# Second pass of a hybrid decoder step: stages that end without GpSimd's drain, the samples' selection in pieces, two expert steps inside the gating's norm

## The reference

```python
proj = x @ w_in                                  # z, xbc, dt, uv, gates
y_a = ssd_branch(z, xbc, dt, ...)                # causal conv, chunked state-space scan, gated RMS norm
u, v = split(gelu(uv)); v = layer_norm(v)        # the gating branch
y_b = u * (tril(w_s) @ v + b_s)                  # spatial gating in chunks of 128 tokens
g_a, g_b = split(sigmoid(gates))
mix = (g_a * (y_a @ w_a) + g_b * (y_b @ w_b)) @ w_out
h = layer_norm(ALPHA * x + mix)
# PEER: 8 heads, product keys: top 16 of 128 on either side, top 16 of their 256 sums
expert, gate = ...                               # 8 * 16 = 128 experts per token, softmax weights
act = gelu(einsum('td,thkd->thk', h, peer_u[expert]))
x = layer_norm(ALPHA * h + einsum('thk,thkd->td', gate * act, peer_v[expert]))
```

## Time and profile before

| | |
|---|---|
| median of 3 runs | 5216.41 us (5214.78 to 5218.38) |
| the profiled execution: first to last instruction (span) | 5205.6 us |
| busy share of the span: PE, PEld, DVE, ACT, POOL | 87, 65, 54, 16, 43% |
| moved by DMA | 1674.51 MB, 322 GB/s over the span |

### The profile page before, as it was taken

One profiled execution on the slowest core, in us unless ns is written; L12 is line 12 of the kernel. 1 busy time (PEld: TensorE's weight loads), 2 busy tenths in 40 slices (PEclk: granted clock), 3 DMA queues, 4 the chain that ended last, 5 costly groups with the idle time before them and its releaser, 6 DMA issues. The chain is left out here.

```text
span 5205.6 us, 48526 instructions
## 1 busy us (share of the span) xinstructions
PE 4523.2 (87%) x18494; PEld 3370.4 (65%) x18494; DVE 2803.0 (54%) x3713; ACT 858.0 (16%) x1941; POOL 2236.7 (43%) x1647
## 2 busy tenths in 40 slices
PE   8999999999999897897789798999857777887776
PEld 6888878888887686776677687787733332332222
DVE  4565622000002678898866665666876655364445
ACT  2333311100000133333301110000111111110000
POOL 3676640000000345454533523455578875364442
PEclk9999999999999998998899899999978899899999
DMA  6766664445554499999999899999999999999998
GB/s 204 228 212 218 199 194 130 139 147 165 165 187 123 125 390 397 417 417 408 403 364 394 338 416 398 397 417 417 376 383 422 421 422 419 382 400 422 421 421 368
DMA packets 331808, 1674.51 MB, mean 322 GB/s; under 512 B 47201, under 2 KB 62113, under 8 KB 195873
## 3 DMA queue, kind: packets, MB, share of 16 engines
q0 software_dynamic: 160640, 1133.71, 53.3%
q1 hardware_dynamic: 165768, 536.51, 30.0%
q10 hardware_dynamic: 5168, 1.19, 0.1%
HBM read 1633.31 MB, written 37.89 MB: 321 GB/s over the span
## 5 line engine op out<-in xcount | busy, mean ns | idle before, releaser
L584 PE MATMUL psum<-rows_a,w_ring 128*128 128x264 f32 x6656 | 1499.2, 387 | 13.7 <-PEq L539 8.9
L584 PEld LDWEIGHTS psum<-rows_a,w_ring 128*128 128x128 f32 x6656 | 1263.3, 191 | 233.9 <-issue 19.0
L584 PE MATMUL psum<-x_and_spare,w_ring 128*128 128x256 f32 x5632 | 1263.6, 385 | 81.9 <-PEq L539 69.1
L584 PEld LDWEIGHTS psum<-x_and_spare,w_ring 128*128 128x128 f32 x5632 | 1080.3, 193 | 251.6 <-issue 92.8
L392 POOL DMA_INDIRECT rows_a<-in_peer_u,expert x384 | 723.7, 1885 | 922.7 <-DVE rows_a L447 857.6
L447 DVE SCALAR_TENSOR_TENSOR rows_a<-rows_a,h_tokens 128x2048 f32<-128x2048 f32 x388 | 889.0, 2293 | 366.4 <-DMA rows_a<-in_peer_u,expert 305.5
L392 POOL DMA_INDIRECT rows_a<-in_peer_v,expert x382 | 506.5, 1326 | 375.6 <-PE psum L491 167.6
L491 PE MATMUL psum<-rows_b,diags 128*128 128x512 f32 x1008 | 483.6, 629 | 193.9 <-ACT diags L481 147.7
L491 PE MATMUL psum<-rows_a,diags 128*128 128x512 f32 x1008 | 488.8, 635 | 149.5 <-ACT diags L481 101.7
L491 PEld LDWEIGHTS psum<-rows_b,diags 128*128 128x128 f32 x1008 | 194.0, 200 | 482.5 <-issue 296.9
L491 PEld LDWEIGHTS psum<-rows_a,diags 128*128 128x128 f32 x1008 | 195.9, 202 | 441.7 <-issue 301.1
(11 more groups left out here) (372 smaller groups left out, 3385.7 us busy)
## 6 DMA issues: line engine op xcount, KB each, us to landing
w_ring<-in_w_tiles SPq DMA_DIRECT2D x896, 512.0 KB
rows_a<-in_state_ssm POOLq DMA_DIRECT2D x32, 512.0 KB, 5.7
out_ssm_sample<-rows_a POOLq DMA_DIRECT2D x32, 512.0 KB, 5.5
rows_a<-acum_rows_dram SPq DMA_DIRECT2D x16, 512.0 KB, 5.0
rows_a<-smp_bc_dram POOLq DMA_DIRECT2D x8, 1024.0 KB, 8.3
acts_by_token<-late SPq DMA_DIRECT2D x16, 512.0 KB, 6.7
branch_b<-acum_rows_dram SPq DMA_DIRECT2D x16, 512.0 KB, 7.5
rows_a<-in_xT SPq DMA_DIRECT2D x3, 2048.0 KB, 18.1
```

What stands on the lines that cost most here:

```text
L584: last = pe.matmul(o, w[:, k * P:(k + 1) * P], x[:, k, :], start=start and k == 0, stop=stop and k == KB - 1)
```

## The change

- In the second pass the stages' blocks are made with `no_gpsimd_drain`, and `clear_sems` is no longer called after them: no clearing, no second barrier. The remaining barrier is made of semaphores alone, the other four engines drain, POOL does not. Several semaphores are no longer made where they are not used.
- In `sgu` the steps of the last v tile, `experts("v", 15)` (2 of the 20), stand behind `ln_centre` on DVE, and the gelu that belongs to them behind `ln_squares` on ACT. POOL's order of gathers is the same.
- In `back` the samples' selection is cut: on DVE `top16` of one side ahead of tiles 1 and 2 each, `ranked` ahead of 3, `places` ahead of 4. POOL's `numbers` is three functions: `key_numbers` at c = 5, `picked_keys` at 6, `pair_numbers` at 7, and the shares at 9 where they were at 6.

```diff
+    def key_numbers(self, o, eng, p):
         o(eng.tensor_copy(self.tif, self.ti[p % 2]))
         o(eng.tensor_scalar(self.tif[:, :, 0, :], self.tif[:, :, 0, :], float(P), None, ALU.mult))
+    def picked_keys(self, o, eng):
+        h4 = self.hot.rearrange("p (b k) i -> p b k i", k=TOPK)
         o(eng.tensor_tensor(h4, h4, mid(self.tif.rearrange("p b s i -> p (b s) i"), 2, TOPK), ALU.mult))
-        for w in (8, 4, 2):
+        o(eng.tensor_tensor(self.hot[:, :, 0:8], self.hot[:, :, 0:8], self.hot[:, :, 8:16], ALU.add))
+    def pair_numbers(self, o, eng):
+        for w in (4, 2):
...
-            self.clear_sems()
+            if ex is None:
+                self.clear_sems()
+            else:
+                self.phase += 1
+
+    def stage_block(self, ex):
+        return self.nc.Block(no_gpsimd_drain=ex is not None)
...
-        with nc.Block() as block:
+        with self.stage_block(ex) as block:
...
-                    experts("v", m)
+                    if m < FT - 1:
+                        experts("v", m)
                 self.ln_squares(act, v, yb, ln)
+                experts("v", FT - 1)
                 self.ln_root(act, ps, root, ln)
...
-                    experts("v", m)
+                    if m < FT - 1:
+                        experts("v", m)
                 self.ln_centre(dve, ps, v, ln)
+                experts("v", FT - 1)
...
-                    if pick and c == 2:
+                    if pick and c == 5:
                         pool.wait_ge(picked, 1)
-                        smp.numbers(o, pool, 0).then_inc(matched, 1)
+                        smp.key_numbers(o, pool, 0)
                     if pick and c == 6:
+                        smp.picked_keys(o, pool)
+                    if pick and c == 7:
+                        smp.pair_numbers(o, pool).then_inc(matched, 1)
+                    if pick and c == 9:
                         pool.wait_ge(inverted, 1)
                         smp.shares(pool, 0, smp.gate).then_inc(smp_chosen, 1)
...
-                    if pick and c == 2:
-                        for s in range(2):
-                            src = self.smp_scores[:, s, :]
-                            smp.top16(o, dve, [src], [smp.spare[:, 0]], [smp.tv[:, 0, s]], [smp.ti[0][:, 0, s]])
+                    if pick and c in (1, 2):
+                        smp.top16(o, dve, [self.smp_scores[:, c - 1, :]], [smp.spare[:, 0]], [smp.tv[:, 0, c - 1]],
+                                  [smp.ti[0][:, 0, c - 1]])
+                    if pick and c == 3:
                         smp.ranked(o, dve, 0, ranked)
+                    if pick and c == 4:
                         dve.wait_ge(ranked, 1)
                         smp.places(o, dve).then_inc(picked, 1)
```

More of the change, by code:

```diff
@@ L957, in ssd @@
         s_in = [self.sem(f"s_state_in{j}") for j in range(2)]
-        conv_in = [self.sem(f"s_conv_in{j}") for j in range(2)]
-        conv_out = [self.sem(f"s_conv_out{j}") for j in range(2)]
+        dord, = S_("dve")
         if ps.smp:
+            bc_turned, bc_ready, bc_out, pord = S_("bc_turned", "bc_ready", "bc_out", "pool")
+            conv_in = [self.sem(f"s_conv_in{j}") for j in range(2)]
+            conv_out = [self.sem(f"s_conv_out{j}") for j in range(2)]
             smp.begin(self, "s")
-        dord, pord = S_("dve", "pool")
         pos = lambda g, t: ps.pos + NT * g + t
         grp = lambda g, t: ps.grp + NT * g + t
-        with nc.Block() as block:
+        with self.stage_block(ex) as block:
             @block.sync
@@ L1395, in _, with ln_sems @@
                         pool.wait_ge(conv_out[j], 16 * (G // 2))
-    def ln_sems(self, name):
-        return {m: self.sem(f"{name}_{m}") for m in ("in", "added", "folded", "mean", "square", "summed", "centred", "root", "inv", "normed")}
+    def ln_sems(self, name, by_vector):
+        return {m: self.sem(f"{name}_{m}") for m in ("in", "mean", "square", "summed", "centred", "root", "inv", "normed")
+                + (("added", "folded") if by_vector else ())}
     def ln_mean(self, pe, ps, v, k, s):
@@ L1482, in sgu @@
         S_ = lambda *names: [self.sem("g_" + m) for m in names]
[L1483 to L1486 removed]
+        w_in, b_in, w0_in, masked, turned, tok_ready, mixed, mix_read = S_(
+            "w_in", "b_in", "w0_in", "masked", "turned", "tok_ready", "mixed", "mix_read")
+        ln = self.ln_sems("vln", ps.smp)
         smp = self.smp if ps.smp else None
@@ L1489, in sgu @@
             smp.begin(self, "g", GT * (G - 1))
-        sq_ready, rms_done, root_ready, smp_done, smp_out = S_("sq_ready", "rms_done", "root_ready", "smp_done", "smp_out")
+            dord, pord, sq_ready, rms_done, root_ready, smp_done, smp_out = S_(
+                "dve", "pool", "sq_ready", "rms_done", "root_ready", "smp_done", "smp_out")
         tb, mb = self.bank[6:8], self.bank[4:6]
-        with nc.Block() as block:
+        with self.stage_block(ex) as block:
             @block.sync
@@ L1613, in _ @@
             def _(dve):
-                o = Chain(dve, dord)
+                o = Chain(dve, dord) if ps.smp else None
                 def experts(key, m):
@@ L1688, in back @@
         S_ = lambda *names: [self.sem("b_" + m) for m in names]
-        keys_in, x_in, xr_out, hs_out, sc_out, merge_done, turned, turn_read = S_(
-            "keys_in", "x_in", "xr_out", "hs_out", "sc_out", "merge_done", "turned", "turn_read")
+        keys_in, x_in, merge_done, turned, turn_read = S_("keys_in", "x_in", "merge_done", "turned", "turn_read")
+        if not ps.last:
+            xr_out, hs_out, sc_out = S_("xr_out", "hs_out", "sc_out")
         ya_in = [self.sem(f"b_ya_in{j}") for j in range(8)]
@@ L1693, in back @@
             "q_ready", "scored", "score_read", "smp_read", "exp_done")
-        smp_exp_done, smp_chosen, smp_in, smp_turned = S_(
-            "smp_exp_done", "smp_chosen", "smp_in", "smp_turned")
+        if pick:
+            smp_exp_done, smp_chosen, smp_in, smp_turned = S_(
+                "smp_exp_done", "smp_chosen", "smp_in", "smp_turned")
         ranked, picked, matched, inverted, dord, pord, aord = S_("ranked", "picked", "matched", "inverted", "dve", "pool", "act")
-        ln = self.ln_sems("hln")
+        ln = self.ln_sems("hln", ps.smp)
         tb, sc = self.bank[6:8], self.bank[4:6]
```

9 lines of the change are left out of this document (3 added, 6 removed).

## The result

| | before | after |
|---|---|---|
| median | 5215.59 us (5204.72 to 5218.38, 4 runs) | 5157.43 us (5156.18 to 5158.54, 4 runs) |
| ratio | | 0.9891 [0.9875, 0.9906] |
| span of the profiled execution | 5205.6 us | 5154.2 us |
| moved by DMA | 1674.51 MB | 1674.51 MB |

So the change makes the kernel about 58 us faster by the medians, 57 by the ratio (49 to 65 by its interval). The forecast was 36 us faster, 5180.4, with a range down to 5171: the direction was right, the gain too small by more than the range allowed. A later series of runs gave the same changed kernel 5152.38 us.

What follows compares the result with a forecast made beforehand. DMA was taken as the bound (7.6 us per tile, PE close at 7.0). Terms 9.0 + 2.1 + 10.4 + 6.7 + 7.8 = 36.0 us off 5216.4 gave 5180.4 us, with an 8-in-10 range of 5171 to 5199.

Steps and rivals of the forecast that it cites:

- end of ssd and end of sgu: Second pass's stage ends without POOL's drain: 9.0 us (between 7.5 and 10.5) at `ssd`, 10.4 us at `sgu`.
- end of back: Everything starts 15.8 us earlier there, but DMA's rest is only 7.8 us, so the gain is 7.8.
- norm of the gating: Norm in `sgu`: inverse 5.5 us earlier (up to 7), but gain taken as DMA's rest of 2.1 us.
- selection: Samples' selection in `back`: cut pieces keep POOL's gathers going; gain 6.7 of 7.2 us of DMA rest.
- Rivals 1 (given back): Removed DMA rest returns at untouched places such as the norm of h; half the gain lost, 5198 us; chance 0.12.
- 2 (only the second barrier): Stage ends: restart after a barrier costs, not POOL's drain; about 1 us per end, 12 us in all, 5204; chance 0.08.
- 3 (too late for SP): Gate tiles in `back`: POOL's shares at c = 9 come too late for SP's loads; slower, 5228 us at 3085; chance 0.03.
- rival 4: End of `ssd`: spatial weights take 30.4 us to land, that end loses about 6 us; 5195 us; chance 0.07.
- the 0 to 3 allowed: End of `ssd`: gathers ahead of the spatial weights eat 0 to 3 us of the 10.5 us shift.
- a rest is length x (1 - share / 1.02): Rule sizing DMA's rests by busy share at the five places the change touches: 41.8 us together.
- the far bound: The five rests counted in bytes, 48.4 us together; less what stays, a gain of 43 at most, 5173 us.
- the 3.5 us allowed: End of `ssd`: DMA rest expected to stay after the change, as the ramp after the start, 3.5 us.

Runs made afterwards that it cites:

- only_norm: The kernel before with only the norm's edit (v's last expert steps behind the centring, their gelu behind the squares): 5197.08 us, ratio 0.9970 to before.
- only_ends: The changed kernel with the norm's and the selection's edits undone, so only the second pass's stage ends are changed: 5174.31 us, ratio 0.9934 to before.

## Why the prediction was wrong

| term | predicted | measured (cleaned stretch) |
|---|---|---|
| end of ssd and end of sgu | 9.0 + 10.4 = 19.4 | 33.2 - 12.2 = 21.0 |
| end of back | 7.8 | 12.2 |
| norm of the gating | 2.1 | 8.1 |
| selection | 6.7 | 11.2 |
| sum | 36.0 | 52.5 |

The five places were read rightly: three ends, a norm and a selection cost time, and DMA rests at each. Nothing was given back at the norm of h: 20 x (1 - 0.47 / 1.02) = 10.8 us of rest from 3652 to 3672, 11.0 before. Rivals 1 (given back), 2 (only the second barrier) and 3 (too late for SP) fell. Of rival 4 a part is true: the spatial weights took 5 us longer to land, not the 0 to 3 allowed, but not 25 either. The Trainium skill, page "DMA: Bandwidth & Descriptors", section "Queues, rings and completion order", has each DMA engine take turns between the queues with work. About twice the 4.9 us is an estimate by that rule; the trace agrees, with 10.0.

The step that failed is the size of the rests, "a rest is length x (1 - share / 1.02)", which came to 41.8 us, with the rule that a place can't give more than its rest. In these traces a DMA engine counted as busy doesn't always move bytes at its full rate. Two windows behind the norm, before:

```profile
2788.00:2796.00 8.00, 8.00 (x42) 7.12 (x41) 5.85 (x6) 0.76 (x2) 3.24 (x2) 1.00 0.98 282
2796.00:2804.00 8.00, 8.00 (x42) 7.12 (x41) 5.75 (x6) 0.76 (x2) 3.74 (x2) 1.00 0.99 354
```

Share 0.98, but 282 GB/s of 416: by share 0.3 us are lost in the first, by bytes 2.6. The prediction stopped its window at 2788, and counted by share inside it. Over the four wide windows shown above the loss removed is 40 us by share (17.1 + 2.7 + 20.4 + 9.6 before, 9.4 + 0.7 after, with full at 1.02) and 49.7 by bytes; 52.5 were measured. By bytes the norm is 7.0 (measured 8.1), the end of `back` 10.6 (12.2), the ends of `ssd` and `sgu` with the selection 20.5 - 12.8 + 24.4 = 32.1 (21.0 + 11.2 = 32.2). The byte count did stand in the prediction, but over narrow windows and only as the far bound. Of the 17 us that the forecast fell short, the wider windows are 4, the bytes 10, and 3 are within the uncertainty.

That sizes the sum; it isn't shown to be the cause at each place. The same two windows have PE busy 8.00 of 8.00 us with 42 matmuls, whether DMA moved 282 or 354 GB/s, and so has every such window up to 2884 (42 or 43 matmuls). In the changed kernel it is the same, 42 matmuls in 8 us at 418 GB/s. So u's tiles go at PE's pace in both, and what the norm gives is PE's earlier start: 7.1 us at the inverse, 7.3 to 8.1 measured for only_norm. The prediction named this ("If PE were the bound in u's tiles it would be 5.5") and set it aside for the 2.1 us. Bytes give 7.0 for the same place, so the size alone doesn't tell the two accounts apart, and no run was made to do it.

Term by term:
- *Ends of ssd and sgu*: right within 2 us, by luck: two errors cancel. By only_ends the end of `ssd` gives 7.2 us up to the gating's inverse (9.0 predicted) and the end of `sgu` 13.1 to 13.5 (10.4 predicted). The shifts are larger, since a stage's end doesn't follow POOL's last gather plus 1.5 us but DVE's last instruction plus 0.47: 13.99 - 0.47 = 13.5 us at the end of `sgu` and not 10.4. Some of it is lost again: only_ends needs 155.4 us from `sgu`'s start to the inverse, 4.5 more than before. And more rest stayed at the end of `ssd` than the 3.5 us allowed: 9.4 by share over the wide window, some 4 of them ahead of the end.
- *End of back*: the gain is smaller than the shift, as predicted (18.2 and 12.2), but larger than the rest of 7.8 that was to bound it; by bytes over the wide window the rest is 10.6. By the runs the gain may be larger still.
- *Norm*: mechanism as predicted and 7.1 us at the inverse, in the text's own span of 5.5 to 7. Counting only the 2.1 us of one window as its worth was the error.
- *Selection*: the text priced POOL's eight instructions as a fixed 17.7 us of work that cutting only spreads. Half of that was waiting beside DVE. Cutting POOL's piece bought nothing that the trace shows (1.4 us); what helped was DVE's cut or POOL's later place.

The 58 us of the first comparison hold, beside the 53 of the edits, a few us of chance from the samples' steps and the first pass, which no part of the prediction had.

## What to carry to other kernels

Where DMA is the bound, price a rest in bytes (length times what is missing in GB/s), over a window whose two edges run at the full rate; here the busy share undercounted it, 40 us against 50. Look also at whether another engine is busy all the time behind the place: there its shift is the gain. A stage that ends with GpSimd's drain while its gathers are under way waited until all of them had landed and some us more, here 10 to 20 us; the barrier of semaphores cost half a us. In a norm on the path, put neither a filler step ahead of the centring nor its activation ahead of the squares, but between them and the root.

## What was not expected of the hardware

- With the drain left out the barrier lets the other engines on in 0.47 us, while POOL's record of the stage's last gather starts only 0.66 us later. With it, POOL stood 20.0 us at the end of `back`, the last 5 to 6 of them with no DMA traffic at all, and the gap at the end of `ssd` was 11.1 us.
- A small GpSimd instruction (the cast of 64x32) took 0.22 us alone and 2.21 us beside DVE's two-input instructions, ten times as much.
- PE's granted clock fell to 0.67 over 10 us in which PE was busy throughout, in a part of the samples' steps that differs between profiles of one kernel; the rest of DMA there was 6.7 to 14.9 us in the 13 traces of kernels with the whole spread.
- A load of 1 MB on SP's queue landed after 4.9 us on idle DMA engines, 10.0 us beside GpSimd's gathers.
